# Roots of the norms spread by transposes of a broadcast column, residual and norm steps tile by tile, low-part products last

## The chip, the cores and the metric

The kernel is written by hand (each engine's queue is an explicit list of instructions with semaphores) and runs on one NeuronCore of a Trainium2 chip. The metric is the device time of one execution in microseconds, the median of several runs. Engines: TensorE (PE), VectorE (DVE), ScalarE (ACT), GpSimd (POOL) and SyncE (SP), which issues most of the loads.

## The reference

Two transformer blocks on x of 512 tokens by 1024 features, in float32. What matters here is how layers join. Four times the kernel computes, with y the output of a sublayer, g and g' gains (in the first block modulated by a conditioning vector):

```python
x = x + gate * rms_norm(y, g_post)           # rms_norm(a, g) = a * rsqrt(mean(a*a) + 1e-6) * g
h = rms_norm(x, g_pre) * (1 + scale) + shift # scale and shift in the first block only
```

The order is: norm of x, mixing sublayer of block 1 (pooling and dilated window attention), the two lines above, conv-FFN, the two lines, the mixing sublayer of block 2 (convolution, block attention, attention to a memory of 256 rows that has a norm of its own, gates), the two lines, conv-FFN, and the first of the two lines.

## The kernel before, in words

Activations lie transposed: features on the 128 partitions, 8 tiles (k = 0 to 7) of 128 x 512, tokens along the free axis. Weights come in units d = 0 to 135 of 256 columns; raw has two buffers (d mod 2). A product keeps float32 accuracy by splitting both operands into a high part (type fp32r) and a low part, the rest: ScalarE copies raw to WH (`split`), GpSimd subtracts to get WL (`cut`), and TensorE issues three matmuls for each (tile, half), high x high, high weight x low activation, low weight x high activation (`product`, line 1690). SyncE loads unit d+2 into the buffer of d once the cut of d is done.

`steps` (lines 443 to 576) is one list in the order of which every engine walks its own handlers, so it sets the order of each queue. `boundary` (line 510) is the part between a sublayer's last product and the next one's first:

1. Column sums. TensorE sums y squared and cross terms of y and x over the features with a stationary tile of squares and a moving column, so the sum of token p of group t stands at partition p, column 4t of PSUM bank 5.
2. `root_y`: ScalarE takes the square root of a column, VectorE the reciprocal, ScalarE makes four copies of the identity scaled by it (L893), and TensorE multiplies them by a matrix of ones (`spread`, L1676), which puts each token's factor on every partition, in bank 4. VectorE also derives from the cross sums the mean square of the new x (lines 1278 to 1282).
3. `root_x`: the same for the new x (L899, L1287, L902), into bank 6.
4. `blend`: for each tile VectorE makes the mix (L1299: y times gain times factor), adds it to x (L1304), and scales the new x (L1312) into dl; the three are staggered over tiles, so that tile k's mix goes with the add of k-1 and the scaling of k-2. ScalarE adds the shift (first boundary only, L920) and copies the high part hH (L922), GpSimd subtracts to hL (L752).
5. `twin` (line 1711): TensorE multiplies the tiles with the first two weight units of the next layer, in `TWIN_ORDER`, which takes the tiles of unit 0 and unit 1 alternately: 16 steps of 6 matmuls. Before a step of unit 0 it waits for hL of that tile.

`warm` issues matmuls of ones by ones into a bank that nothing reads: fillers while TensorE would be idle. Units of BY_ROWS (the two of each twin) are split and cut in two parts (tiles 0 to 3, 4 to 7); `("split", v + 2, 1)` is the second part of unit 1.

The first boundary lies at 277 to 326 us, the second at 676 to 714, the third at 1254 to 1296. The first norm (`norm`, around 36 to 42 us) and that of the memory (983 to 994) have no column sums: TensorE multiplies the squares by the full matrix of ones (L1642, so that all partitions hold all sums), VectorE picks each token's own with the identity and a reduction (L1343, L1345), and after the root scales four identities (L1350). Behind a boundary into a FFN, ScalarE's loop `up` waits for the first half of unit 0 (`pe_seg`), loads a function table, takes the bias (L1023) and splits the next unit; the twin is followed by TensorE's loop over the other units.

## Time and profile before

| | us |
|---|---|
| median of 3 runs (lowest, highest) | 1664.28 (1662.15, 1668.35) |
| the profiled execution's own time | 1666.63 |
| its span | 1664.8 |
| TensorE busy | 1555.7 (93%) |
| ScalarE, VectorE, GpSimd busy | 664.9, 588.2, 713.9 |
| TensorE's mean granted clock (share of full) | 0.967 |

### The profile page before, as it was taken

How to read it: one execution, taken by the hardware profiler on the slowest of the kernel's cores; microseconds unless marked ns; L12 is line 12 of the kernel's file. 1: busy time of each engine (PE TensorE's matmuls, PEld its weight loads, DVE VectorE, ACT ScalarE, POOL GpSimd, SP SyncE). 2: the span in 40 equal slices, each digit the busy share in tenths (PEclk: the TensorE clock that was granted, in tenths of full speed). 3: DMA queues.
4: the chain of work that ended last, by engine and by line, in shares of the span. 5: the costliest groups of instructions: out<-in, count | busy, mean ns of one | idle time of the engine just before them, and what ended most of it. 6: DMA issues, size and time to landing. Idle time of an engine off the chain costs nothing.

```text
span 1664.8 us, 19895 instructions
## 1 busy us (share of the span) xinstructions
PE 1555.7 (93%) x7670; PEld 1260.4 (76%) x7670; DVE 588.2 (35%) x928; ACT 664.9 (40%) x987; POOL 713.9 (43%) x608
## 2 busy tenths in 40 slices
PE   7899978899999999999989889999899999999996
PEld 4699757688888888788855568787687788887885
DVE  3665442523333100422034430342325555555001
ACT  2442453444444322322344443453333555544231
POOL 0467103535545544545411136335524554455442
PEclk8999987999999999999999999999999999999999
DMA  8463015322232223234210123122311222322221
GB/s 368 159 271 141 27 68 110 82 98 82 94 101 88 85 86 95 76 102 135 84 45 30 38 102 115 51 76 80 132 55 51 86 90 101 101 81 83 90 86 65
DMA packets 28491, 162.73 MB, mean 98 GB/s; under 512 B 4584, under 2 KB 4840, under 8 KB 13704
## 3 DMA queue, kind: packets, MB, share of 16 engines
q1 hardware_dynamic: 24960, 151.05, 26.4%
q10 hardware_dynamic: 3464, 10.74, 2.5%
q8 instruction: 47, 0.77, 0.2%
q14 instruction: 20, 0.16, 0.0%
HBM read 157.04 MB, written 4.74 MB: 97 GB/s over the span
## 4 chain that ended last, share of the span: by engine, by line
PE 70%; issue 10%; POOL 8%; DVE 6%; DMA 3%; ACT 2%; POOLq 0%; SPq 0%; ACTq 0%; DVEq 0%
PE ps L1693 60%; POOL WL L774 7%; DMA adaw<-w_ada_dram 2%; PE ps L1659 1%; PE ps L1902 1%; DMA raw<-w_up_dram 1%; PE ps L1916 1%; PE ps L1929 1%; DVE S L1584 1%; POOL WL L738 1%; DVE ps L1299 1%; DVE S L1571 1%; PE ps L1826 1%; DVE xT L1304 1%; DVE md L1574 0%
## 5 line engine op out<-in xcount | busy, mean ns | idle before, releaser
L738 POOL TENSOR_TENSOR WL<-raw,WH 128x512 fp32r<-128x512 f32 (+2 forms) x344 | 369.7, 1103 | 584.2 <-ACT WH L854 584.1
L1693 PE MATMUL ps<-hH,WH 128*128 128x512 f32 x1136 | 461.1, 406 | 22.2 <-POOL hL L752 9.3
L1693 PE MATMUL ps<-hL,WH 128*128 128x512 f32 x1136 | 453.9, 400 | 0.0
L1693 PE MATMUL ps<-hH,WL 128*128 128x512 f32 x1136 | 453.4, 399 | 0.0
L774 POOL TENSOR_TENSOR WL<-raw,WH 128x512 fp32r<-128x512 f32 x176 | 246.3, 1430 | 253.9 <-ACT WH L1014 253.9
L1693 PEld LDWEIGHTS ps<-hH,WH 128*128 128x128 f32 x1136 | 216.8, 191 | 79.5 <-issue 25.3
L1693 PEld LDWEIGHTS ps<-hH,WL 128*128 128x128 f32 x1136 | 216.6, 191 | 53.2
L1693 PEld LDWEIGHTS ps<-hL,WH 128*128 128x128 f32 x1136 | 216.8, 191 | 50.4
L854 ACT ACTIVATE WH<-raw 128x1024 fp32r<-128x1024 f32 (+3 forms) x172 | 148.1, 885 | 234.8 <-PE ps L1693 231.2
L1693 PE MATMUL ps<-hidH,WH 128*128 128x512 f32 x352 | 137.9, 392 | 1.1 <-POOL WL L774 1.1
L1693 PE MATMUL ps<-hidL,WH 128*128 128x512 f32 x352 | 137.0, 389 | 0.0
L1693 PE MATMUL ps<-hidH,WL 128*128 128x512 f32 x352 | 136.9, 389 | 0.0
L1470 DVE SCALAR_TENSOR_TENSOR act<-ps,vec,act 128x511 f32<-128x511 f32 x66 | 49.4, 748 | 173.2 <-ACT act L1023 173.2
L1014 ACT ACTIVATE WH<-raw 128x2048 fp32r<-128x2048 f32 x44 | 84.1, 1910 | 60.7 <-PE ps L1693 60.7
L1023 ACT ACTIVATE act<-ps,vec 128x512 f32<-128x512 f32 x66 | 50.1, 778 | 87.0 <-PE ps L1693 86.7
L1693 PEld LDWEIGHTS ps<-hidH,WH 128*128 128x128 f32 x352 | 66.1, 188 | 15.2 <-POOL WL L774 1.8
L1493 DVE TENSOR_TENSOR hidL<-act,hidH 128x512 f32 x44 | 70.1, 1631 | 21.2 <-ACT hidH L1043 21.2
L1693 PEld LDWEIGHTS ps<-hidH,WL 128*128 128x128 f32 x352 | 66.1, 188 | 13.8
L1693 PEld LDWEIGHTS ps<-hidL,WH 128*128 128x128 f32 x352 | 66.1, 188 | 13.4
L1571 DVE SCALAR_TENSOR_TENSOR S<-ps,W 128x128 f32<-128x128 f32 (+3 forms) x32 | 15.7, 491 | 127.5 <-PE ps L1902 127.5
L1023 ACT ACT_TABLE_LOAD x22 | 28.2, 1283 | 76.6 <-DVE hidL L1493 53.7
L1693 PE MATMUL ps<-WH,hpH 128*128 128x256 f32 x192 | 54.8, 285 | 0.8 <-DVE hpL L1374 0.5
(275 smaller groups left out, 2221.9 us busy)
## 6 DMA issues: line engine op xcount, KB each, us to landing
raw<-w_up_dram SPq DMA_DIRECT2D x44, 1024.0 KB, 4.9
raw<-w_in_dram SPq DMA_DIRECT2D x36, 1024.0 KB, 4.9
adaw<-w_ada_dram SPq DMA_DIRECT2D x20, 1024.0 KB, 7.1
raw<-w_down_dram SPq DMA_DIRECT2D x16, 768.0 KB, 4.2
raw<-w_down_dram SPq DMA_DIRECT2D x16, 640.0 KB, 3.9
adap<-w_ada_dram SPq DMA_DIRECT2D x4, 1024.0 KB, 18.1
xT<-x_dram ACTq DMA_DIRECT2D x2, 2048.0 KB, 10.2
raw<-w_mem_kv_dram SPq DMA_DIRECT2D x4, 1024.0 KB, 4.7
```

What stands on the lines that cost most here:

```text
L738: pool.tensor_tensor(WL[:, d % 2, ks, cols], raw[:, d % 2, ks, cols], WH[:, d % 2, ks, cols].bitcast(F32), ALU.subtract).then_inc(lo_done, 1)
L774: pool.tensor_tensor(WL[:, half, k:k + 2, :], raw[:, half, k:k + 2, :], WH[:, half, k:k + 2, :].bitcast(F32), ALU.subtract).then_inc(lo_do ...
L854: sc.activation(WH[:, d % 2, 0:nk, cols], raw[:, d % 2, 0:nk, cols], ACT.Copy).then_inc(hi_done, 1)
L1014: sc.activation(WH[:, half, :, :], raw[:, half, :, :], ACT.Copy).then_inc(hi_done, 2)
L1023: sc.activation(act[:, 2 * half + m, :], ps[:, 2 * half + m, :], ACT.Identity, bias=b, scale=w2).then_inc(seeded, 1)
L1299: ve.scalar_tensor_tensor(out=ps[:, 5 + 2 * (k % 2), :], in0=outputs[n][:, k, :], scalar=post_gains[n][:, k:k + 1], in1=ps[:, 4, :], op0=A ...
L1304: ve.tensor_tensor(xT[:, i, :], xT[:, i, :], ps[:, 5 + 2 * (i % 2), :], ALU.add).then_inc(x_added[0], 1)
L1470: ve.scalar_tensor_tensor(out=t[:, 1:S], in0=z[:, 0:S - 1], scalar=w1, in1=t[:, 1:S], op0=ALU.mult, op1=ALU.add).then_inc(dve_own, 1)
L1493: ve.tensor_tensor(hidL[:, bass.ds(j * 2 + m, 1), :], act[:, m:m + 1, :], hidH[:, bass.ds(j * 2 + m, 1), :].bitcast(F32), ALU.subtract).th ...
L1571: ve.scalar_tensor_tensor(out=S2[:, n % 2, 0:w], in0=ps[:, 4 + n % 2, 0:w], scalar=DH ** -0.5, in1=bias, op0=ALU.mult, op1=ALU.add).then_i ...
L1584: ve.tensor_scalar(S2[:, n % 2, 0:w], S2[:, n % 2, 0:w], md2[:, 2, n:n + 1], None, ALU.mult).then_inc(p2_scaled, 1)
L1693: mm = pe.matmul(out, lhs[x], rhs[y], start=(first and i == 0), stop=(last and i == 2))
```

## The change

- `norm`, first norm and memory: the sums are now columns too (`squares` uses a tile of squares as the stationary operand and one column of ones); ScalarE takes the root straight from PSUM, scale and epsilon in the same instruction, VectorE the reciprocal.
- All spreads: instead of scaled identities and ones, TensorE transposes the column of factors, read as 128 x 128 by repeating it, four transposes (two for the memory).
- `boundary`: the filler before the first spread goes, that before the blend has 4 matmuls, not 8; at the end of the kernel the filler before the spread goes.
- The second part of the split and cut of unit 1 moves from before the blend into it, on both engines behind tile 2.
- `blend` on VectorE: mix, add and scaling of one tile follow each other.
- `first_products`: in the twins and in the first units of the first and of the memory norm, each step issues its four matmuls with hH first, and only then waits for hL and issues the two with hL; the two halves of the unit so end one matmul apart.

```diff
-                    ("root_y", n), ("warm", 4, v + 1), ("spread_y", n), ("root_x", n), ("warm", 2, v + 1), ("spread_x", n),
-                    ("evac_y", n, KD - 1), ("split", v + 2, 1), ("warm", 8, v + 1), ("blend", n, nxt)]
+                    ("root_y", n), ("spread_y", n), ("root_x", n), ("warm", 2, v + 1), ("spread_x", n),
+                    ("evac_y", n, KD - 1), ("warm", 4, v + 1), ("blend", n, nxt)]
...
             def blend(n, nxt):                                    # GpSimd
                 for k in range(KD):
+                    if k == 3:
+                        cut(STAGE[n][1] + 1, 1)
...
-                sc.wait_ge(ry_ready, b)
-                for t in range(TT):
-                    ins = sc.activation(nt[:, 0, t * P:(t + 1) * P], ident, ACT.Identity, scale=ry_t[:, t:t + 1])
-                ins.then_inc(diag_y, 1)
...
             def norm(n):                                          # ScalarE
                 c = norm_source[n][1] // P
-                sc.wait_ge(var_ready, WHOLE[n] + 1)
-                sc.activation(nt[:, 0, 4:4 + c], nt[:, 0, 0:c], ACT.Sqrt).then_inc(std_ready, 1)
+                sc.wait_ge(weights_ready, 2)
+                sc.wait_ge(ss_added, KD * (SQUARED[n] + 1))
+                sc.activation(nt[:, 0, 0:c], ps[:, 5, 0:4 * c].rearrange("p (t i) -> p t i", i=4)[:, :, 0], ACT.Sqrt,
+                              bias=eps, scale=1.0 / D).then_inc(std_ready, 1)
 
             def blend(n, nxt):                                    # ScalarE
-                apply(nxt)
+                apply(nxt, 0, 3)
+                split(STAGE[n][1] + 1, 1)
+                apply(nxt, 3, KD)
...
+                for k in range(KD):                               # VectorE, blend
+                    d, m = output_tile(n, k)
+                    ve.wait_ge(banks_read[pair_of(d)], bank_use(d) + 1)
+                    ve.scalar_tensor_tensor(out=ps[:, 5 + 2 * (k % 2), :], in0=outputs[n][:, k, :], scalar=post_gains[n][:, k:k + 1],
+                                            in1=ps[:, 4, :], op0=ALU.mult, op1=ALU.mult).then_inc(mix_ready, 1)
+                    ve.wait_ge(mix_ready, KD * b + k + 1)
+                    ve.tensor_tensor(xT[:, k, :], xT[:, k, :], ps[:, 5 + 2 * (k % 2), :], ALU.add).then_inc(x_added[0], 1)
+                    ve.wait_ge(x_added[0], KD * b + k + 1)
+                    if k == 0:
+                        ve.wait_ge(rx_spread, b + 1)
+                    if k >= 4:
+                        wait_h(ve, nxt, k - 4)
+                    ve.scalar_tensor_tensor(out=dl[:, k % 4, :], in0=xT[:, k, :], scalar=gains[nxt][:, k:k + 1],
+                                            in1=ps[:, 6, :], op0=ALU.mult, op1=ALU.mult).then_inc(scaled, 1)
...
             def spread(n, i):                                     # TensorE
-                pe.wait_ge((diag_y, diag_x)[i], RESID[n] + 1)
+                pe.wait_ge((ry_ready, rx_ready)[i], RESID[n] + 1)
                 for t in range(TT):
-                    mm = pe.matmul(ps[:, 4 + 2 * i, t * P:(t + 1) * P], ones[:], nt[:, i, t * P:(t + 1) * P], start=True, stop=True)
+                    mm = pe.transpose(ps[:, 4 + 2 * i, t * P:(t + 1) * P], (ry_t, rx_t)[i][:, t:t + 1].broadcast_to([P, P]), ident)
...
+            def first_products(outs, s, n, k, last):
+                hi, lo = (memH, memL) if n == N_MEM else (hH, hL)
+                cols = [slice(m * P, (m + 1) * P) for m in range(2)]
+                pe.wait_ge(h_hi, KD * SPLITS[n] + k + 1)
+                for o, c in zip(outs, cols):
+                    pe.matmul(o, WH[:, s, k, c], hi[:, k, :], start=(k == 0), stop=False)
+                    pe.matmul(o, WL[:, s, k, c], hi[:, k, :], start=False, stop=False)
+                wait_h(pe, n, k)
+                done = [pe.matmul(o, WH[:, s, k, c], lo[:, k, :], start=False, stop=last) for o, c in zip(outs, cols)]
+                return done
```

## Rows read from the trace of the kernel before

**Rows 1.** The page, chain that ended last: shares by engine.
```profile
PE 70%; issue 10%; POOL 8%; DVE 6%; DMA 3%; ACT 2%; POOLq 0%; SPq 0%; ACTq 0%; DVEq 0%
```

**Rows 2.** Timeline of TensorE, third boundary: start, duration, instruction, [idle before, releaser].
```profile
1258.45 1.03 PE L1670 MATMUL ps<-small,prod 128*128 128x1 f32 x8
...
1260.47 1.16 PE L1676 MATMUL ps<-nt,ones 128*128 128x128 f32 x8
...
1267.94 0.76 PE L1693 MATMUL ps<-hH,WH 128*128 128x512 f32 x1 [2.81 <-POOL hL L752]
...
1295.68 0.79 PE L1693 MATMUL ps<-hH,WH 128*128 128x512 f32 x1 [3.56 <-POOL WL L774]
```

**Rows 3.** Timeline of ScalarE, third boundary.
```profile
1259.14 1.28 ACT L893 ACTIVATE nt<-ident_t,small 128x128 f32<-128x128 f32 x4 [0.25 <-DVE small L1273]
...
1265.80 0.63 ACT L922 ACTIVATE hH<-dl 128x512 fp32r<-128x512 f32 x1 [2.25 <-DVE dl L1312]
...
1285.96 1.28 ACT L1023 ACT_TABLE_LOAD   x1 [8.03 <-PE ps L1693]
```

**Rows 4.** Timeline of VectorE, third boundary.
```profile
1260.00 0.16 DVE L1282 TENSOR_TENSOR small<-ps,small 128x4 f32<-128x4 f32 x1
1260.63 0.18 DVE L1287 RECIPROCAL small<-small 128x4 f32<-128x4 f32 x1 [0.48 <-ACT small L899]
1261.66 1.41 DVE L1299 SCALAR_TENSOR_TENSOR ps<-y,vec,ps 128x512 f32<-128x512 f32 x2 [0.85 <-PE ps L1676]
...
1265.03 0.74 DVE L1312 SCALAR_TENSOR_TENSOR dl<-xT,vec,ps 128x512 f32<-128x512 f32 x1
```

**Rows 5.** Timeline of GpSimd, third boundary.
```profile
1263.63 2.50 POOL L731 TENSOR_TENSOR WL<-raw,WH 128x512 fp32r<-128x512 f32 x2 [2.62 <-ACT WH L848]
1266.51 1.28 POOL L752 TENSOR_TENSOR hL<-dl,hH 128x512 fp32r<-128x512 f32 x1 [0.38 <-ACT hH L922]
```

**Rows 6.** Timeline of TensorE, first and second boundary.
```profile
285.09 1.85 PE L1670 MATMUL ps<-small,prod 128*128 128x1 f32 x8
...
325.78 0.74 PE L1693 MATMUL ps<-hH,WH 128*128 128x512 f32 x1 [3.60 <-POOL WL L774]
...
689.91 0.47 PE L1693 MATMUL ps<-hH,WH 128*128 128x512 f32 x1 [2.81 <-POOL hL L752]
```

**Rows 7.** Timeline of TensorE, transposes of the first attention (half clock, then full).
```profile
215.42 2.25 PE L1837 MATMUL ps<-ident_t,S 128*128 128x128 f32 x8 [6.25 <-DVE S L1444]
...
220.92 0.66 PE L1837 MATMUL ps<-ident_t,S 128*128 128x128 f32 x4
```

**Rows 8.** Timeline of VectorE, first and second boundary.
```profile
287.45 0.16 DVE L1282 TENSOR_TENSOR small<-ps,small 128x4 f32<-128x4 f32 x1
...
680.96 0.16 DVE L1282 TENSOR_TENSOR small<-ps,small 128x4 f32<-128x4 f32 x1
```

**Rows 9.** Timeline of VectorE, end of the kernel: a mix and the add that needs it.
```profile
1654.19 0.75 DVE L1329 SCALAR_TENSOR_TENSOR ps<-yff,vec,ps 128x512 f32<-128x512 f32 x1
1654.98 0.69 DVE L1332 TENSOR_TENSOR xT<-xT,ps 128x512 f32<-128x512 f32 x1
```

**Rows 10.** Windows: PE, PEld, DVE, ACT, POOL busy (instructions), granted clock, DMA share, GB/s.
```profile
286.00:289.00 3.00, 3.00 (x15) 3.00 (x15) 0.68 (x4) 2.16 (x8) 0.23 (x1) 0.50 0.49 54
...
1268.00:1271.00 3.00, 3.00 (x7) 2.38 (x8) 3.00 (x6) 0.98 (x2) 1.95 (x2) 0.50 0.74 303
```

**Rows 11.** Timeline of TensorE, memory norm (three rows) and first norm (last row).
```profile
984.10 4.93 PE L1642 MATMUL ps<-sq,ones 128*128 128x256 f32 x16 [1.45 <-ACT sq L862]
991.21 1.03 PE L1649 MATMUL ps<-nt,ones 128*128 128x128 f32 x4 [2.19 <-DVE nt L1350]
994.02 0.55 PE L1693 MATMUL ps<-bufAH,WH 128*128 128x256 f32 x1 [1.78 <-DVE bufAL L1366]
...
39.53 2.08 PE L1649 MATMUL ps<-nt,ones 128*128 128x128 f32 x8 [1.27 <-DVE nt L1350]
```

**Rows 12.** DMA issues from 240 to 330 us: count, KB each, median us to landing.
```profile
raw<-w_up_dram SPq DMA_DIRECT2D x5, 1024.0 KB, 16.7
```

More of the change, by code:

```diff
@@ L1641, in squares @@
                 pe.wait_ge(sq_ready, KD * SQUARED[n] + k + 1)
-                pe.matmul(ps[:, 5, 0:w], ones[:], sq[:, k % 2, 0:w], start=(k == 0), stop=(k == KD - 1)
-                          ).then_inc(ss_added, 1)
+                for t in range(w // P):
+                    mm = pe.matmul(ps[:, 5, 4 * t:4 * t + 1], sq[:, k % 2, t * P:(t + 1) * P], ones[:, 0:1],
+                                   start=(k == 0 and t == 0), stop=(k == KD - 1 and t == w // P - 1))
+                mm.then_inc(ss_added, 1)
             def norm(n):
-                pe.wait_ge(diag_ready, WHOLE[n] + 1)
+                if n == N_PRE1:
+                    pe.wait_ge(ident_loaded, 16)
+                pe.wait_ge(inverse_ready, WHOLE[n] + 1)
                 for t in range(norm_source[n][1] // P):
-                    mm = pe.matmul(ps[:, 4, t * P:(t + 1) * P], ones[:], nt[:, 1, t * P:(t + 1) * P], start=True, stop=True)
+                    mm = pe.transpose(ps[:, 4, t * P:(t + 1) * P], nt[:, 0, 8 + t:9 + t].broadcast_to([P, P]), ident)
                 mm.then_inc(rstd_ready, 1)
@@ L1719, in twin @@
                         pe.wait_ge(lo_done, 4 * d + k // 2 + 1)
-                    if w == 0:
-                        wait_h(pe, nxt, k)
-                    for m in range(2):
-                        cols = slice(m * P, (m + 1) * P)
-                        mm = product(ps[:, 2 * w + m, :], (WH[:, w, k, cols], WL[:, w, k, cols]),
-                                     (hH[:, k, :], hL[:, k, :]), k == 0, k == KD - 1)
+                    for mm in first_products([ps[:, 2 * w + m, :] for m in range(2)], w, nxt, k, k == KD - 1):
                         if k == KD - 1:
@@ L1766, in seg @@
                         if d in first_of:
-                            wait_h(pe, first_of[d], k)
-                        for half in (0, 1) if d in first_of else (m,):
-                            cols = slice(half * P, (half + 1) * P)
-                            mm = product(ps[:, 2 * p + half, 0:w], (WH[:, s, k, cols], WL[:, s, k, cols]),
+                            first, mm = first_products([ps[:, 2 * p + i, 0:w] for i in range(2)], s, first_of[d], k, k == nk - 1)
+                            if k == nk - 1:
+                                first.then_inc(pe_seg, 1)
+                        else:
+                            cols = slice(m * P, (m + 1) * P)
+                            mm = product(ps[:, 2 * p + m, 0:w], (WH[:, s, k, cols], WL[:, s, k, cols]),
                                          (src[0][:, k0 + k, :], src[1][:, k0 + k, :]),
                                          k == 0 and q == 0, k == nk - 1 and (not down or q == 3))
-                            if d in first_of and k == nk - 1 and half == 0:
-                                mm.then_inc(pe_seg, 1)
                 else:
```

49 lines of the change are left out of this document (5 added, 44 removed).

## The prediction

> **What bounds the kernel now.** I read the page's chain of waits first, then each engine's timeline around the places that the diff touches. TensorE carries 70% of the chain [rows 1]. So a change pays only where TensorE has to wait for the vector work between two layers, and the reader is to look at three boundaries (post-norm into next pre-norm), at the memory norm, the first norm and the end.
>
> At the third boundary TensorE does its last column sums at 1258.45 (ending 1259.48), a filler step, the first spread at 1260.47, then more filler and the second spread, and then nothing until the first real product at 1267.94, released by GpSimd's low part [rows 2]. Behind it lies a chain: root and four copies of the identity scaled by the root on ScalarE (1.28 us), first mix on VectorE at 1261.66, first normalised tile at 1265.03, its high part at 1265.80, its low part at 1266.51 [rows 2 to 5]. From 1267.94 the 96 products of the twin run without a hole until 1292.12 (1295.68 less 3.56 of idling) [rows 2]. The first boundary ends alike, with 3.60 us idle before 325.78; at the second the products start at 689.91 [rows 6].
>
> **The change part by part.**
>
> *Spreads.* The four ScalarE copies go (1.28 us each root), and so does the filler ahead of the first spread; four matmuls in two passes (8 records, 1.16 us) become four transposes. The diff's own transpose of a broadcast column is not in the trace; the nearest rows are transposes of ordinary tiles: four take 0.66 us at full clock, and eight 2.25 us, so 1.12 for four, at half clock [rows 7]. Bounds for four: 0.6 (ordinary) to 2.3 (the old spread's eight records at half clock, twice 1.16); I take 0.66 and 1.12.
>
> *Where mixing starts.* VectorE still needs the x root in program order: the sum is ready when the instruction of 1260.00 ends (1260.16); ScalarE, no longer busy with copies, takes the root at once (0.3), the reciprocal 0.18 (as at 1260.63) [rows 4]; the first mix starts at 1260.70, not 1261.66. The spread, 1259.48 to 1260.14, is no longer what it waits for. At the other boundaries the same instruction starts at 287.45 and 680.96 [rows 8], which gives first mixes at 288.16 and 681.66.
>
> *Three steps in a row.* A dependent step starts 0.79 us after the one before it (1654.19 to 1654.98), an independent one 0.66 (half of the pair of 1.41 at 1261.66, less overlap) [rows 4, 9]. Mix, add, scale of one tile then begin 0.79 and 0.72 apart, and the next tile 0.66 later: a period of 2.17 us against 1.92 before. The first scaled tile starts 1.51 after the first mix, against 3.37 before (1261.66 to 1265.03) [rows 4]. So it starts at D = 1262.2 (was 1265.03) and 683.2 at the second; at the first the x spread at half clock holds it to 290.1 (sums end 286.94 [rows 6], then 1.12, four filler records 0.96, 1.12). The last tile starts 15.2 after D, near 1277.4, about a microsecond later than before; TensorE's order needs it only at D+18, so that costs nothing as long as TensorE is behind.
>
> By the Trainium skill, page "VectorE: DVE Perf Modes", section "The DRAIN you can't avoid", a pipe empties after each instruction whatever one does and "the semaphore costs nothing extra here". By that the period would stay at 1.92 and the time fall by about another 0.4 us a boundary; the 0.79 against 0.66 of this trace says otherwise, and I go by the trace.
>
> *Products with low parts last.* Four of six products of a tile need only the high part. It is ready at D+1.45 (the 0.77 from 1265.03 to 1265.80, plus 0.63), the low part at D+2.85 (GpSimd 1.28) [rows 3 to 5]; before, TensorE started 2.91 after D. First and third boundary pay a price: the first tile's half signals one product pair later (2 x 0.23 = 0.5 us), and ScalarE's table load at 1285.96 waits for that signal [rows 3].
>
> *The second cut moved into the blend.* GpSimd's 2.50 us [rows 5] comes after its third low part (D+7.2), so the fourth is ready at D+11.0, the fifth 12.3, the sixth 13.6, the last 18.0. ScalarE's copy (1.05) fits in its gaps. Behind the cut wait the load of the next-but-one weights (the buffer comes free at about D+9.7) and four low parts.
>
> *TensorE against this supply.* At 0.233 us a product, 1.4 a step: first step D+1.5 to 3.4 (waits 0.4 for the low part), then 4.8, 6.2, 7.7, 9.1; the step of the fourth tile has its high products by 10.0 and waits 1.0 for the cut, ends 11.5; the other 10 steps run through to D+25.5. Before, the twin lasted 24.2 from 1267.94, of which 1.5 is a stretch at half clock, 0.50 in 1268 to 1271 after the idle time [rows 2, 10]. If such a stretch comes early again, the wait for the cut absorbs it, so the sum doesn't lean on the clock.
> - third: 1262.2 + 25.5 = 1287.7 against 1292.1: 4.4, less 0.5 for the signal: 3.9
> - second: 683.2 + 25.5 = 708.7 against 689.91 + 24.1 = 714.0: 5.3 (no signal price; there ScalarE waits for both halves)
> - first: a shift on ScalarE adds 0.77 to each tile: 290.1 + 26.3 = 316.4 against 322.2: 5.8, less 0.5: 5.3
>
> Together 14.5. The FFN and projection loops behind are kept full by TensorE, so the start carries to the end.
>
> *Memory norm.* Squares run as columns (4.93 us now, my estimate 0.5 less); then TensorE idles 2.19 for three VectorE steps, a root and the scaled identities, spreads in 1.03 and waits 1.78 more [rows 11]. Now the root follows the squares directly, behind the table load (1.28, [rows 3]) that ScalarE does anyway: 0.9 earlier; two transposes save 0.4; starting on the high part 0.7. Together 2.5 with the squares; I take 2.4 (0.9 to 3.3).
>
> *First norm.* The spread at 39.53 waits 1.27 for VectorE [rows 11]. Without it TensorE goes on at 38.3 and spreads by 39.4, not 41.6: 2.2. The row product behind then has more of its 7.5 us at half clock: 1.3 left (0 to 2.2).
>
> *The end.* The copies (1.28) and 0.5 of the spread go: 1.8.
>
> **Sum:** 14.5 + 2.4 + 1.3 + 1.8 = 20.0 us. The profiled execution took 1666.63 (span 1664.8), which gives 1646.6; it lies 2.4 above the median of 1664.28, and with the same gain the median becomes 1644.3. I say 1644.5.
>
> **Rivals.**
> *A: the clock.* 3 us windows show half clock from 286 to 289 although TensorE was busy 3.00 of 3.00 with column sums and fillers [rows 10]; so it is half (1.2 of 2.4 GHz) for all that work, and the diff leaves 12 of 28 filler records and 8 of 16 spread records a boundary. If the twins begin with a longer stretch at half clock than the waits absorb, each further 3.1 us costs 1.45: three boundaries 4.4, time 1649. Against it: the idle gap shrinks from 2.81 to about 1.2.
> The Trainium skill ("TensorE: Matmul & The Clock Gate", section "PE-mode transpose") says that transposes don't count as busy for the clock; by that this rival gets likelier. Transposes between other matmuls ran at full clock here (0.66 for four [rows 7]), which neither shows nor refutes it.
> *B: a late load.* At the first boundary the load freed by the moved cut (290.1 + 10.5 = 300.6) meets the bias rows' store; with the 16.7 us that such loads took there [rows 12] it is there at 317.3, just as ScalarE wants it (about 317.4); I expect less, since the store is over by then. Any more comes off the 5.3: time up to 1650.
> *C: slower.* Half clock through the whole twins: 96 products at 0.427 instead of 0.233 are 18.6 us each, 56 for three; 56 less 20 gives 1700. It decides from the point where 36% of each twin (20/56) is slow. For it: the half-clock row above; against it: in each boundary before, the clock came back some 3 us after products flowed.
> *D: the gains don't add.* Only the spreads' shortening survives (about 1 us at each of three first mixes, the norms 3.7, the end 1.8: 8.5), since GpSimd's cut sets the twin's end, later than I think: 1655.8.
>
> **How the numbers follow.** Main case 68%, A 14%, B 8%, D 6%, C 4%. Main alone 1641 to 1648 (memory 0.9 to 3.3, first 0 to 2.2, one less slow stretch a boundary). The range goes to 1653 to take in A and B, and to 1640. Half a percent is 8.3 us, about what a measurement tells from none: below 1656 lie main, A, B and some of D: 0.90; same 0.06; slower 0.04.
>
> **What would show it.** TensorE's first product at D+1.5 (1.5 before its low part) and its largest hole in the twin at the fourth tile, some 1 us, released by GpSimd's low part; VectorE's mixes 2.17 apart; ScalarE's table load 4 to 5.5 us earlier from the start of its boundary; four records per spread. Wrong if four transposes take over 1.5 us at full clock, if half clock is seen beyond D+7, or if the first loop step stalls on a load.

## The result, and the profile after

The changed kernel takes 1648.2 us in the median of four runs (1646.7 to 1649.7) and the kernel before 1665.2 on the same chip (1662.2 to 1668.4). The ratio is 0.989, with a 95% interval of 0.987 to 0.991. The two profiled executions took 1666.63 and 1646.69 us, with spans of 1664.8 and 1644.9: 19.9 us apart where the medians are 17.0 apart. The forecast was 1644.5 us (1640 to 1653), with a sum of 20.0 for the profiled pair; it had started from a median of 1664.3 for the kernel before.

The page of the changed kernel: busy time of each engine, and the chain by engine (it answers [rows 1]).

```profile
PE 1548.0 (94%) x7644; PEld 1256.5 (76%) x7644; DVE 585.0 (36%) x917; ACT 656.3 (40%) x959; POOL 714.3 (43%) x608
...
PE 70%; issue 10%; POOL 9%; DVE 6%; DMA 3%; ACT 2%; POOLq 0%; SPq 0%; ACTq 0%; DVEq 0%
```

The chain is made of the same engines in nearly the same shares. So the page alone tells nothing of where 20 us went, and one has to go into the three boundaries.

Timeline of TensorE at the third boundary, changed kernel (answers [rows 2]; times are 14 us earlier, since that much had been gained before it).

```profile
1245.07 0.63 PE L1656 MATMUL ps<-ident_t,small 128*128 128x128 f32 x4
...
1246.48 1.11 PE L1656 MATMUL ps<-ident_t,small 128*128 128x128 f32 x4 [0.34 <-DVE small L1281]
1247.38 1.92 PE L1668 MATMUL ps<-ones 128*128 128x128 f32 x8
1249.39 0.70 PE L1682 MATMUL ps<-hH,WH 128*128 128x512 f32 x1
...
1258.79 0.74 PE L1685 MATMUL ps<-hL,WH 128*128 128x512 f32 x2 [0.70 <-POOL hL L751]
...
1277.55 0.79 PE L1673 MATMUL ps<-hH,WH 128*128 128x512 f32 x1 [4.03 <-POOL WL L773]
```

A spread is four records now. The first takes 0.63 us for all four, at full clock; the second comes behind a wait of 0.34 us and takes 1.11, at half clock, and so does the filler behind it. The forecast had both at full clock here. The only hole inside the twin products is at the fourth tile, released by GpSimd's low part. Ahead of the FF loop TensorE idles 4.03 us, where it was 3.56.

ScalarE at the same boundary (answers [rows 3]); the first row is the root of the y norm, from which I count every stretch below.

```profile
1244.35 0.26 ACT L887 ACTIVATE small<-ps,small 128x4 f32<-128x4 f32 x1 [0.20 <-PE ps L1639]
...
1248.62 0.63 ACT L916 ACTIVATE hH<-dl 128x512 fp32r<-128x512 f32 x1 [1.92 <-DVE dl L1299]
...
1267.83 1.28 ACT L1017 ACT_TABLE_LOAD   x1 [3.38 <-PE ps L1685]
```

VectorE (answers [rows 4]): the x root's reciprocal, then mix, add and scale of the first tile, and the next tile's mix.

```profile
1246.24 0.18 DVE L1281 RECIPROCAL small<-small 128x4 f32<-128x4 f32 x1 [0.37 <-ACT small L893]
1246.34 0.74 DVE L1290 SCALAR_TENSOR_TENSOR ps<-y,vec,ps 128x512 f32<-128x512 f32 x1
1247.11 0.69 DVE L1293 TENSOR_TENSOR xT<-xT,ps 128x512 f32<-128x512 f32 x1
1247.84 0.75 DVE L1299 SCALAR_TENSOR_TENSOR dl<-xT,vec,ps 128x512 f32<-128x512 f32 x1
1248.50 0.75 DVE L1290 SCALAR_TENSOR_TENSOR ps<-y,vec,ps 128x512 f32<-128x512 f32 x1
```

GpSimd (answers [rows 5]): low part of tile 0 (tiles 1 and 2 follow at 2.17 us steps), the moved cut, the first two low parts behind it.

```profile
1249.33 1.29 POOL L751 TENSOR_TENSOR hL<-dl,hH 128x512 fp32r<-128x512 f32 x1 [2.61 <-ACT hH L916]
...
1254.93 2.55 POOL L728 TENSOR_TENSOR WL<-raw,WH 128x512 fp32r<-128x512 f32 x2
1257.44 2.55 POOL L751 TENSOR_TENSOR hL<-dl,hH 128x512 fp32r<-128x512 f32 x2
```

The spacings 0.77, 0.73 and 0.66 add up to the forecast period of 2.17 us (1248.50 less 1246.34 is 2.16), and D, the start of the first scaled tile, is 1247.84: with the 14.3 us gained before it, the forecast's 1262.2 becomes 1247.9.

TensorE at the first and second boundary (answers [rows 6]).

```profile
285.65 1.09 PE L1656 MATMUL ps<-ident_t,small 128*128 128x128 f32 x4
...
290.87 0.47 PE L1682 MATMUL ps<-hH,WH 128*128 128x512 f32 x1 [0.71 <-ACT hH L916]
...
300.27 0.73 PE L1685 MATMUL ps<-hL,WH 128*128 128x512 f32 x2 [0.70 <-POOL hL L751]
...
319.06 0.79 PE L1673 MATMUL ps<-hH,WH 128*128 128x512 f32 x1 [4.06 <-POOL WL L773]
...
678.99 0.77 PE L1682 MATMUL ps<-hH,WH 128*128 128x512 f32 x1 [0.40 <-ACT hH L916]
```

TensorE at the first norm (first row), the memory norm (three rows) and the end (last row): these answer [rows 11] and, for the end, the filler and spread of the kernel before.

```profile
38.05 1.09 PE L1629 MATMUL ps<-ident_t,nt 128*128 128x128 f32 x4
...
973.02 5.16 PE L1619 MATMUL ps<-ones,sq 128*128 128x1 f32 x32 [1.45 <-ACT sq L861]
978.99 0.69 PE L1629 MATMUL ps<-ident_t,nt 128*128 128x128 f32 x2 [0.81 <-DVE nt L1325]
980.79 0.55 PE L1682 MATMUL ps<-bufAH,WH 128*128 128x256 f32 x1 [1.11 <-ACT bufAH L916]
...
1632.91 0.65 PE L1656 MATMUL ps<-ident_t,small 128*128 128x128 f32 x4 [0.57 <-DVE small L1267]
```

**Where the 19.9 us came from.** I lay the two traces side by side at equal landmarks and note how far the changed kernel is ahead: 1.14 us before the first boundary, 6.72 at the first loop's start (gain 5.58), 5.65 at the end of the projections behind that loop (a loss of 1.07), 10.96 behind the second boundary (5.3), 13.88 behind the memory norm (2.8), 14.28 before the third boundary (0.4), 18.13 at the second loop's start (3.86), 18.10 at the loop's end, 19.9 at the end of the span (1.8). The loss of 1.07 is the one entry that no term of the forecast has. Windows of the changed kernel behind the first loop's start show what it is (columns as in [rows 10]).

```profile
319.00:321.00 2.00, 1.95 (x5) 1.58 (x6) 2.00 (x2) 0.16 (x1) 2.00 (x2) 0.50 0.52 86
...
323.00:325.00 2.00, 2.00 (x6) 1.57 (x5) 0.00 (x0) 0.00 (x0) 1.79 (x2) 0.53 0.10 37
```

The granted clock is 0.50 (1.2 of 2.4 GHz) for some 5.7 us behind the idle stretch. The kernel before has 0.52 and 0.63 in the two windows behind its own loop start, then 1.00:

```profile
325.78:327.78 2.00, 2.00 (x5) 1.63 (x6) 2.00 (x2) 0.11 (x1) 2.00 (x2) 0.52 0.54 94
327.78:329.78 2.00, 2.00 (x8) 1.54 (x7) 0.13 (x1) 0.00 (x0) 2.00 (x2) 0.63 0.95 397
```

### The profile page after: what moved, and what is told of

Read it like the earlier page. It is cut to its first block, busy times and chain, and to the rows that moved or that the text cites. A ratio compares the mean times of both kernels' runs of the same rounds, so it can differ in the third digit from the quotient of the medians.

```text
span 1644.9 us, 19792 instructions
## 1 busy us (share of the span) xinstructions
PE 1548.0 (94%) x7644; PEld 1256.5 (76%) x7644; DVE 585.0 (36%) x917; ACT 656.3 (40%) x959; POOL 714.3 (43%) x608
## 4 chain that ended last, share of the span: by engine, by line
PE 70%; issue 10%; POOL 9%; DVE 6%; DMA 3%; ACT 2%; POOLq 0%; SPq 0%; ACTq 0%; DVEq 0%
PE ps L1673 58%; POOL WL L773 7%; DMA adaw<-w_ada_dram 2%; PE ps L1639 1%; PE ps L1889 1%; DMA raw<-w_up_dram 1%; PE ps L1903 1%; PE ps L1916 1%; DVE S L1560 1%; POOL WL L735 1%; DVE dl L1299 1%; DVE xT L1293 1%; DVE ps L1290 1%; PE ps L1813 1%; PE ps L1685 1%
## 5 line engine op out<-in xcount | busy, mean ns | idle before, releaser
L1673 PE MATMUL ps<-hH,WH 128*128 128x512 f32 x1024 | 414.6, 405 | 10.0 <-POOL WL L773 8.1
L1673 PE MATMUL ps<-hL,WH 128*128 128x512 f32 x1024 | 407.7, 398 | 0.0
L1673 PE MATMUL ps<-hH,WL 128*128 128x512 f32 x1024 | 407.6, 398 | 0.0
L1673 PEld LDWEIGHTS ps<-hH,WH 128*128 128x128 f32 x1024 | 194.7, 190 | 61.1 <-issue 15.6
L1673 PEld LDWEIGHTS ps<-hH,WL 128*128 128x128 f32 x1024 | 194.2, 190 | 47.7
L1673 PEld LDWEIGHTS ps<-hL,WH 128*128 128x128 f32 x1024 | 194.7, 190 | 45.2
```

Of the source, the lines that this page charges most:

```text
L1673: mm = pe.matmul(out, lhs[x], rhs[y], start=(first and i == 0), stop=(last and i == 2))
```

## The experiments

A kernel's timed runs here spread over 3 to 7 us, and two medians of the unaltered changed kernel, taken at different times, are 1648.2 and 1646.3. Parts worth 1 to 3 us can't be read from that. So I read each experiment in its trace, over three stretches that begin at the root of the y norm on ScalarE: to the first product of the FF loop at the first and third boundary, to the first product behind the twins at the second. In us:

```
                    first   second  third   end    median
before              40.52   34.33   37.05   14.3   1665.2
changed             34.94   29.01   33.20   12.5   1648.2
changed again       34.94   29.02   33.20   12.5   1646.3
low part first      34.45*  29.95   33.68   12.5   1647.1
staggered steps     37.08   31.19   34.55   12.7   1649.2
scaled identities   37.08   32.11   35.77   15.3   1658.6
cut before          33.32*  28.75   32.94   12.5   1645.5
old norms           34.93   29.00   33.20   12.5   1648.2
no fillers          34.01*  29.32   33.54   12.5   1646.1
first half early    33.64   29.57   31.93   12.5   1647.4
best, no filler     33.66   28.76   31.93   12.5   1643.8
best, filled        32.70*  28.75   31.93   12.5   1636.3
```

"End" is from the last y root to the end of the span. At a star TensorE did the last column sums at 2.4 GHz and not at 1.2: the x root came 1.56 instead of 2.38 us after the y root, and D, the start of the first scaled tile, 3.49 instead of 4.44. So 0.95 us of the difference at a star is the clock's, and a part is read there from D on. The unaltered kernel repeats its stretches within 0.01 us.

**The changed kernel again.**

> The changed kernel, unaltered, beside the others on the same chip: 1648 us in the median, 17 us (1.0%) under the kernel before. Everything below is told against this run.

Measured: 1646.3 us in the median of four, ratio 0.989 (0.986 to 0.991).

**Low part first.**

```
-  wait(high k); for o, c: WH*hi, WL*hi
-  wait(low k);  for o, c: WH*lo
+  wait(high k); wait(low k)
+  for o, c: WH*hi, WH*lo, WL*hi
```

> One part undone: the product with a tile's low part is no longer last. Each first product again waits for high and low part of its tile, and then goes high*high, high*low of the operand, low*high of the weights for each half, as before. Main theory (the part is worth the distance between a tile's high and low part, once per boundary, because the tiles arrive slower than TensorE uses them up and the last tile ends the stretch): the first product of a boundary starts 1.4 us later (D+2.85 in place of D+1.45, D the start of the first scaled tile); at the end of the stretch 0.9 us of it is left at each of three boundaries, less the 0.5 us by which the signal after the first half comes earlier in this order at two of them, and 0.7 us at the memory norm: 2.4 us in all over the changed kernel, 1650.5 us. Rival (TensorE never waits for a low part except at the fourth tile, and what is late at the end is the weights' cut, not the tile): no change, within 0.5 us. Rival of the clock: a longer idle stretch ahead of the first product makes the half-clock stretch behind it longer, and each boundary costs 1 to 2 us more than the main theory says: 5 to 7 us.

Measured, first product of the third boundary:

```profile
1251.50 0.47 PE L1683 MATMUL ps<-hH,WH 128*128 128x512 f32 x1 [1.64 <-POOL hL L751]
```

The first product waits for GpSimd and starts 1.37 us later after the y root than in the changed kernel (1251.50 less 1245.09, against 5.04). The stretches are 0.94 longer at the second and 0.48 at the third; at the first it is 0.46, counted from D. From the spread of the memory norm to its first product it is 2.47 in place of 1.80. Together 2.5 us, where the main theory had 2.4. The rival (no change) falls. The clock rival falls too: nothing near 2 us is added at a boundary. The median is only 0.7 above the unaltered one, and the trace shows why totals can't tell. In this execution the first FF loop ran at 2.4 GHz from its start and took 352.3 us to the next y root, not 354.8; but from 840 to 854 us, in work that the change doesn't touch, the granted clock was 0.50 and 0.54 where the changed kernel had 1.00, and nearly 5 us went there.

**Staggered steps.**

```
-  for k: mix k; add k; scale k
+  for k in range(KD + 2): mix k; add k-1; scale k-2
```

> One part undone: VectorE's three steps of a tile (mix, add of the residual, scale) are staggered over the tiles again, as before, so that no step directly follows the one it depends on. Main theory: the first scaled tile comes 1.86 us later (two mixes, two adds ahead of it in place of one each), the period of a tile falls from 2.17 to about 1.92 us, so that the eighth tile comes near where it did, and the twin products end about 1.4 us later at each boundary, since TensorE starts 1.9 us later and makes up only part of it: 4.2 us in all, 1652.3 us. Rival (only the last tile matters, the period's gain pays for the later start): within 0.5 us of the changed kernel. Rival of the clock as in the run before: the longer idle stretch adds another 1 to 2 us per boundary.

Measured, third boundary:

```profile
1252.32 0.47 PE L1689 MATMUL ps<-hH,WH 128*128 128x512 f32 x1 [1.95 <-ACT hH L916]
```

The first product is 1.86 us later after the y root, as worked out (6.90 against 5.04). The third stretch grows by 1.35, near the 1.4 of the theory, the second by 2.18 and the first by 2.14: 5.7 in all against 4.2. The larger two are the clock's: idle for 2.42 us ahead of the first product at the first boundary, TensorE ran at half clock from 291.8 to 295.2 us (high products of 0.63 us in place of 0.40); at the second the granted clock is 0.83 over the 10 us from 680. The rival "only the last tile matters" falls. So each theory had a part: 1.4 from the order, and 0.8 more where a slow stretch followed that the waits for tiles did not absorb. An idle stretch of this length doesn't always bring one: at the third boundary TensorE had idled for 1.95 us, and the products ran at full clock.

**Scaled identities.**

```
-  transpose(ps, ry[:, t:t+1].broadcast_to([P, P]), ident)
+  ScalarE: nt[:, t, :] = ident * ry[:, t:t+1]      (4 copies)
+  TensorE: matmul(ps, ones, nt[:, t, :])
```

> One part undone: the roots of the residual norms are spread by scaled identities (ScalarE writes four of them, TensorE multiplies them by ones) in place of the transposes of a broadcast column, at the three boundaries and at the end; first norm and memory norm stay as changed, and nothing is added to the filler products. Main theory: ahead of the first mix this costs 0.96 us at the third boundary, about 2 us and 2.4 us at the second and first (their ones products run at the half clock), and 1.8 us at the end, all of it on the path that sets the start of the mixes: about 7 us in all, 1655 us. Rival (the spread of the roots is hidden behind VectorE's other work at the boundaries, only the end shows it): 1.8 us. Rival: the scaled identities keep TensorE idle longer, the clock falls in the boundary where it did not, and the sum is over 9 us.

Measured, third boundary: the two spreads, and the windows.

```profile
1251.38 1.73 PE L1667 MATMUL ps<-nt,ones 128*128 128x128 f32 x8 [0.99 <-ACT nt L894]
...
1253.75 1.75 PE L1667 MATMUL ps<-nt,ones 128*128 128x128 f32 x8
```

```profile
1249.00:1252.00 3.00, 2.01 (x17) 1.93 (x17) 1.20 (x7) 2.31 (x8) 2.50 (x2) 0.97 0.00 0
1252.00:1255.00 3.00, 3.00 (x16) 3.00 (x15) 1.44 (x2) 1.51 (x5) 0.00 (x0) 0.50 0.00 0
```

The stretches are 2.14, 3.10 and 2.57 longer and the end 2.72: 10.5 us, and the median is 12.3 higher (ratio to the kernel before 0.996, 0.995 to 0.998). The main theory said 7, "over 9 because TensorE idles and its clock falls" was the second rival, and that it is: without the filler ahead of the y spread TensorE waits 0.99 us for ScalarE's copies, and both spreads run at half clock, 1.7 us each, where the kernel before had 1.16 [rows 2]. The kernel before, its y root and its filler:

```profile
1258.63 0.26 ACT L889 ACTIVATE small<-ps,small 128x4 f32<-128x4 f32 x1 [0.20 <-PE ps L1659]
```

```profile
1259.34 1.14 PE L1688 MATMUL ps<-ones 128*128 128x128 f32 x8
```

Its filler delayed nothing: with it the y spread starts at 1260.47, 1.84 us after the root, and here without it also 1.84 after (1251.38 less 1249.54), since both wait for the copies. It bought full clock for both spreads. So 10.5 us is not the share of the transposes in the 20: this experiment takes them out without giving the filler back. Their share is better read up to the first mix, which starts 5.33, 4.04, 3.04 and 3.04 us after the y root in the kernel before (three boundaries and the end) and 2.80, 1.99, 1.99 and 1.22 in the changed one: 7.5 us, the 7 of the main theory, and still the largest part.

**The cut ahead of the blend.**

```
   root_x, spread_x, evac_y(last),
+  split and cut of the second half,
   blend:
-     behind tile 2 (the third): split and cut of the second half
```

> One part undone: the second half of the next weights' split and its cut by GpSimd stand ahead of the mixes again, not behind the third tile. Counted from the start of the root of the y norm on ScalarE, where the changed kernel takes 34.94 us to the first product of the FF loop at the first boundary, 29.0 us to the end of the twin products at the second and 33.20 us at the third. Theory (the move is worth nothing: the hole of 0.70 us before the fourth tile's low part goes, but the first low part comes about a microsecond later, as ScalarE's 1.05 us and GpSimd's 2.55 us are then ahead of it, and the tile rate of 2.17 us sets the end either way): each stretch within 0.3 us of the changed kernel's. Rival (the cut ahead of the blend keeps GpSimd from the first low parts, and this is carried through): 1 to 2.5 us more per boundary. Rival (the hole is lost time that comes back in full): 0.7 us less per boundary. In the total all three lie within 0 to +7 us, and only the first is no change.

Measured: 0.26 us less at the second and third boundary. At the first it is 1.62 less, of which 0.95 is the clock of the column sums. The other 0.67 is not: in both traces the granted clock is 1.00 from the first product of the first boundary on. First product and wait for the first low part there, and the same wait at the third boundary:

```profile
286.98 0.47 PE L1678 MATMUL ps<-hH,WH 128*128 128x512 f32 x1 [0.85 <-ACT hH L912]
...
288.38 0.73 PE L1681 MATMUL ps<-hL,WH 128*128 128x512 f32 x2 [0.23 <-POOL hL L749]
```

```profile
1248.25 0.73 PE L1681 MATMUL ps<-hL,WH 128*128 128x512 f32 x2 [0.98 <-POOL hL L749]
```

The hole at the fourth tile goes everywhere, 0.70 us, but the first low part comes 0.85 us later. At the third boundary TensorE waits 0.98 us for it; at the first, where the first product itself starts later after D, only 0.23, and the hole comes back nearly in full. So the theory (nothing, within 0.3) stands at the second and third boundary, and the second rival (0.7 back in full) at the first, in one execution. Moving the cut into the blend bought nothing and lost 1.2 us over the three. The first rival falls.

**The old norms.**

```
   first norm and memory norm:
-  column sums [128x1], root, reciprocal, transposes
+  sums into a full bank [128xw], fix-up, root, scaled identities * ones
```

> One part undone: first norm and memory norm are summed and spread as before (sums by ones into a full bank, VectorE's fix-up, four or two scaled identities by ones); the order with the low part last stays, and the boundaries stay as changed. Main theory: at the first norm the first product comes 1.2 us later, at the memory norm the first product comes 1.9 us later (in the kernel before, from the start of the sums' last record to the first product: 2.19 us of waiting and 1.03 us of ones products, where the changed kernel has 0.81 and 0.69, and before that sums of 128x256 in place of 128x1): 3 us in all. Rival (what is late at the memory norm is the cut of the weights and not the norm, the gain that was seen there came from the clock): under 1 us at the memory norm, 1.2 us in all.

Measured, the two spreads.

```profile
39.51 2.08 PE L1636 MATMUL ps<-nt,ones 128*128 128x128 f32 x8 [1.27 <-DVE nt L1337]
...
980.60 1.21 PE L1636 MATMUL ps<-nt,ones 128*128 128x128 f32 x4 [2.19 <-DVE nt L1337]
```

Memory norm: from the end of the sums to the first product it is 4.51 us in place of 2.61, so 1.9 as expected. But the sums themselves take 4.93 us here and in the kernel before, at a granted clock of 1.00, and 5.16 to 6.55 us as one-column products in the other twelve traces, with a mean clock of 0.54 to 0.87 over them. So the new form gives back 0.2 to 1.6 us of its gain, more or less from one execution to the next. First norm: the spread ends 2.45 later (41.59 against 39.14), and the first product behind the next row product 2.2 to 3.4 later than in the three runs beside it. That is about twice the 1.2 expected: I had let the row product's half-clock stretch take a microsecond back, and here it didn't. The rival (under 1 us at the memory norm) falls.

**No fillers at the boundaries.**

```
-  ("root_x", n), ("warm", 2), ("spread_x", n), ("evac_y", n, 7), ("warm", 4), blend
+  ("root_x", n), ("spread_x", n), ("evac_y", n, 7), blend
```

> One thing taken away that the change touched in its place and count: TensorE's filler products between the two spreads and behind the second, at the three boundaries (nothing reads them). Counted as in the runs beside it, from the root of the y norm. Theory (TensorE is idle there anyway, the fillers are hidden and only guard the clock, which falls at the first boundary with them too): 0 to 0.5 us more per boundary, all of it from transposes and first products at the half clock. Rival (the fillers are what keeps the clock at 2.4 GHz at the second and third boundary): there the granted clock in the 6 us behind the first product is near 0.5 to 0.7, where the changed kernel has about 1.0, and the stretch is 1.4 us or more longer at each. Rival (the fillers delay the x spread or the first product): 0.3 to 0.5 us less per boundary.

Measured, third boundary (TensorE busy 0.14 of 2 us, then products at half clock for 4 us).

```profile
1244.00:1246.00 2.00, 0.14 (x1) 0.17 (x2) 1.93 (x4) 0.63 (x1) 0.21 (x1) 0.50 0.02 4
...
1248.00:1250.00 2.00, 2.00 (x6) 1.52 (x6) 1.97 (x3) 0.57 (x2) 1.25 (x1) 0.53 0.00 0
```

0.31 us more at the second and 0.34 at the third boundary; at the first no difference (0.02), counted from D. The first product starts where it did, 5.04 after the y root. The clock is indeed worse, as the first rival says, but it costs 0.3 and not 1.4: VectorE delivers a tile each 2.17 us, so that the products wait for the fourth tile's low part anyway (0.70 us in the changed kernel); in this trace that hole is gone, and the slow products have filled it and most of what else TensorE waits. This is what I had called absorption, measured.

**The first unit's first half earlier.**

```
-  ..., (0, 6), (1, 3), (0, 7), (1, 4), ...      last tile: both halves high, both low
+  ..., (0, 6), (0, 7), (1, 3), (1, 4), ...      last tile: half 0 high, low, signal; half 1
```

> One thing added to the changed kernel: of the twin products at a boundary, the last tile of the first unit is taken one step earlier in the order, (0,7) ahead of (1,3), and at a unit's last tile the first half's three products (and its signal) stand ahead of the second half's. What the first product of the FF loop waits for is a chain that begins at that signal (table load, two evacuations, the split on ScalarE, the cut on GpSimd) and took 9.7 us in the changed kernel, with TensorE idle for 4.0 us at its end. A sum over the rows of the changed kernel (tile k's high part at D+1.5+2.17k, its low part 1.4 us after, the cut of 2.55 us behind the third, 0.2335 us for a product) gives the signal at D+18.34 in place of D+19.73, and the last twin product at D+26.05 in place of D+25.57. Theory (the chain sets the loop's start): at the first and third boundary 1.4 us less (33.5 and 31.8 us), TensorE's idle time before the loop about 2.2 us, at the second boundary, which has no such chain behind it, 0.5 us more (29.5 us); in all 2.3 us less. Rival (the chain is held by the second unit or by VectorE, not by this signal): no change at the first and third, 0.5 us more at the second. Rival of the clock: the shorter idle stretch leaves TensorE's clock up, and the first loop steps run up to 2.5 us faster, twice.

Measured, first loop product of the third boundary:

```profile
1278.31 0.79 PE L1673 MATMUL ps<-hH,WH 128*128 128x512 f32 x1 [2.21 <-POOL WL L773]
```

Stretches 33.64, 29.57 and 31.93, idle time 2.21: expected were 33.5, 29.5, 31.8 and 2.2. What the loop's start waits for is the chain behind that signal, not TensorE. The clock rival falls: both loops still start with 3.3 us at half clock. The median did not show the 2 us (1647.4), and neither did the profiled execution, which had the slow clock at 841.5 to 855 us as in the run with the low part first (granted clock 0.50 over 847 to 855).

**Two probes of the clock.** TensorE idles before 36.3 us at the start of the kernel, at 1.2 GHz. In the one probe it transposes there, in the other it multiplies.

```
+  for _ in range(40): transpose(ps[:, 7, 0:P], ident, ident)
   or
+  for _ in range(20): matmul(ps[:, 7, 0:P], ones, ones)
```

> A probe of the clock in the changed kernel: in the idle stretch of TensorE at the start (about 31.7 to 36.3 us, the granted clock there is 1.2 GHz) 40 transposes of the identity are issued; nothing reads them. They take 0.27 us each at 1.2 GHz and 0.16 at 2.4 (from 1.09 and 0.65 us for four). Theory A (transposes leave the clock as it is): all 40 run at 1.2 GHz, 10.9 us, and what follows starts about 6 us later than in the changed kernel. Theory B (they raise it as products do): the granted clock reaches 1.00 within them, as in the twin probe with products, and 40 take under 9 us. The Trainium skill (TensorE: Matmul & The Clock Gate, the section on the PE-mode transpose) states A.

> The twin of the probe with transposes: at the same place 20 ordinary fp32 products of ones by ones (128x128, 40 records, since each leaves two). A record takes 0.24 us at 1.2 GHz and 0.12 at 2.4. Both theories: the granted clock rises to 2.4 GHz within them after 4 to 7 us, and the 40 records take 6 to 8 us. If the clock stays at 1.2 GHz here too (9.6 us), the probe tells nothing on transposes.

Measured, transposes, then products, each with windows.

```profile
32.52 6.80 PE L1673 MATMUL ps<-ident_t 128*128 128x128 f32 x40
```

```profile
34.00:36.00 2.00, 2.00 (x12) 2.00 (x11) 1.93 (x3) 0.00 (x0) 1.43 (x2) 0.50 1.00 422
36.00:38.00 2.00, 2.00 (x15) 2.00 (x15) 0.52 (x3) 0.00 (x0) 0.00 (x0) 0.73 1.02 430
38.00:40.00 2.00, 2.00 (x22) 2.00 (x20) 0.00 (x0) 0.00 (x0) 0.00 (x0) 1.00 1.00 422
```

```profile
29.72 6.23 PE L1673 MATMUL ps<-ones 128*128 128x128 f32 x40
```

```profile
32.00:34.00 2.00, 2.00 (x17) 2.00 (x16) 0.82 (x2) 0.00 (x0) 0.62 (x1) 0.78 1.03 434
34.00:36.00 2.00, 1.95 (x18) 1.75 (x16) 1.93 (x3) 0.00 (x0) 0.00 (x0) 1.00 0.99 422
```

Nothing but transposes runs on TensorE from 32.5 to 39.2, and the clock goes from 0.50 to 1.00 within them, near 37 us; with the products it does so near 33. That is theory B. TensorE had been busy with one-column products at half clock before, in both probes, and had not idled. Each probe ran once. The forecast had weighed the Trainium skill's rule ("TensorE: Matmul & The Clock Gate", section "PE-mode transpose") that transposes don't count for the clock; for these fp32 transposes the trace disagrees.

**The best version, filled and not.** Both kernels have the cut ahead of the blend at all boundaries and the earlier signal at the first and third. They differ only in this:

```
   twin(d0)
+  for _ in range(9): matmul(ps[:, 7, 0:P], ones, ones)
   FF loop
```

> Three things on the changed kernel: the earlier signal of the first unit's first half at the first and third boundary (at the second the old order), the split and cut ahead of the blend at all three, and nine filler products (ones by ones, 18 records, about 2.1 us at 2.4 GHz, nothing reads them) behind the twin products, in the idle stretch before the FF loop's first product at the first and third boundary. From the runs so far: 1.3 us less at each of first and third boundary by the signal, 0.26 us less at each of three by the cut, 3.3 us in all by these two. Theory of the clock (the half-clock stretch at the head of each FF loop, 3.3 to 5.6 us long in the traces, follows from the idle stretch of 2.2 to 4.1 us before it): with the fillers the granted clock is 1.00 in the first 6 us of both loops, worth 1.7 us each against the same kernel without fillers: 6.5 to 7 us under the changed kernel, 1640 us. Rival (ones by ones does not hold the clock, or the clock falls later in the loop all the same): no gain by the fillers, 1643.5 us. Rival (the fillers delay the loop's first product): up to 0.5 us more per loop.

> The run above without its filler products: the earlier signal at the first and third boundary and the cut ahead of the blend at all three. Counted from the root of the y norm: 33.4 us at the first boundary, 28.75 at the second, 31.65 at the third (the changed kernel: 34.94, 29.0, 33.2), the head of each FF loop at 1.2 GHz for about 3.3 us. In the total 3.3 us under the changed kernel, 1644 us; rival (the cut ahead of the blend and the earlier signal do not add, because tile and not cut sets the seventh tile's low part): 2.6 us.

Measured, filled kernel: fillers and first loop product of the third boundary, and the window behind it.

```profile
1267.20 2.17 PE L1860 MATMUL ps<-ones 128*128 128x128 f32 x18
1269.57 0.49 PE L1671 MATMUL ps<-hH,WH 128*128 128x512 f32 x1 [0.20 <-POOL WL L773]
```

```profile
1270.00:1272.00 2.00, 2.00 (x11) 1.59 (x10) 1.73 (x4) 0.12 (x1) 1.80 (x2) 1.00 0.68 164
```

The kernel without fillers, first loop:

```profile
316.32:318.32 2.00, 2.00 (x5) 1.62 (x6) 1.54 (x2) 0.82 (x2) 2.00 (x2) 0.53 0.56 102
```

Without fillers: 1643.8 us (ratio 0.987, 0.985 to 0.989), stretches 33.66, 28.76, 31.93. Against the changed kernel 2.8 us in the stretches: the rival's number (2.6), since behind the earlier signal the cut's place adds nothing at the first and third boundary. With fillers: 1636.3 us, ratio 0.984 (0.982 to 0.985), the fastest of all. Both loops run at 1.00 from the first product and are 1.52 us shorter each (352.3 against 353.8, 353.5 against 355.0), close to the 1.7 expected. That is 3.0 of the 6.4 us between the two profiled executions; the other 3.4 lie in places that the fillers don't touch (1.6 before the first boundary, 1.0 in it, by the clock of the column sums, 0.8 between the second and the third), and whether they would come back in each run stays open. The medians are 7.5 apart, of five runs each (1634.2 to 1639.4 against 1638.3 to 1645.0); the traces account for 3.0 of that.

## Why the prediction was right

The total came out as 20.0 forecast and 19.9 measured for the profiled pair. The terms bear that out one by one, but that the sums meet to a tenth is luck: the parts gave 0.5 us more than the terms, 0.4 us more came between the memory norm and the third boundary, where no term is, and 1.07 us were lost at the head of the first loop, which no term has either.

**Spreads as transposes.** Taken at 0.66 us for four at full clock and 1.12 at half; measured 0.63 to 0.65, and 1.06 to 1.11. A broadcast column as the stationary side costs nothing extra.

**Where mixing starts.** Third boundary: forecast 1260.70, less 14.28 is 1246.42; measured 1246.34. At the first the x spread sets D, as said, but 0.4 earlier (288.55 against 290.1 less 1.14), because groups of four half-clock records follow each other 0.86 us apart, not 1.12: the rows' durations overlap.

**Three steps in a row.** Period 2.17 forecast and measured; the experiment puts the part at 1.35 us where the clock is quiet.

**The drain.** By the Trainium skill ("VectorE: DVE Perf Modes", section "The DRAIN you can't avoid"), where the semaphore costs nothing extra, the period would have stayed at 1.92. The trace gave 2.17, as [rows 9] had said.

**The twin products.** First product at D+1.55, hole at the fourth tile 0.70 (said: about 1.0), twin's end at D+25.7 (said: 25.5; at the first boundary D+26.4 against 26.3). A slip in it had no effect: five low parts stand behind the cut, not four. ScalarE's table load came 5.6 us earlier after the y root at the first boundary and 3.9 at the third (said: 4 to 5.5). From it 9.72 us to the loop at the third boundary and 9.74 at the first, as in the kernel before (9.72 and 9.75), so no load came late (rival B).

**The boundaries** together: 5.58 + 5.3 + 3.86 = 14.7 against 14.5. **Memory norm** 2.8 against 2.4, with one term wrong: the column sums are not 0.5 shorter than the old ones but 0.2 longer in this execution (5.16 against 4.93), and up to 1.6 in others. **First norm** 1.14 at the first boundary against 1.3, though for the wrong reason: the part itself is worth about 2.5, and a stretch at half clock between 167 and 172 us took 1.6 of it back in this execution. **End** 1.8 against 1.8. The sum of these is 20.5. The parts undone one at a time come to about 22 us (2.5, 5.7, 10.5, less 1.2, and 1.9 + 2.5 for the norms); they are not independent, as the scaled identities without their filler show.

**What the forecast didn't have** is the 1.07 lost at the head of the first loop. I had seen that the signal came later in relation to the twin's end and charged its 0.5 us, but not that TensorE's idle time there grows by the same amount (3.60 to 4.06) and that a half-clock stretch follows it. How long this is differs from execution to execution: to the next y root the first loop takes 352.3 us in one of thirteen traces, 353.8 in five and 354.8 in seven, with nothing changed in it. The kernel before had 353.8 and the changed one 354.9 (the fillers of the best version give 352.3). It does not look like chance alone. Of the 18 loops that had 4.03 to 4.07 us of idle time ahead of them, 12 began with 5 to 5.8 us at half clock; of the 8 with 2.2 to 3.6 us, none did (seven had about 3.3 us, one none). That speaks for the longer idle stretch as part of the price of the change, about 1.1 us in two loops of three, though no run varies it alone; in the profiled execution only the first loop paid it.

**The clock (rival A)** is most likely what lies between 19.9 and 17.0, and in the 3.7 us by which the median missed 1644.5; that is not shown. What speaks for it: long executions go with a low clock (the kernel before, seven runs: 1657.6 us at a mean granted clock of 0.971, 1668.2 at 0.963), and two medians of the changed kernel are 2 us apart. It never cost what rival A charges in the boundaries: in the changed kernel the first products ran at half clock for at most a microsecond, and where they did so for longer, without the fillers, the waits for tiles took up all but 0.3 us. By its letter one sign of being wrong did occur, half clock beyond D+7; it was at the head of the loops, behind the twins, where the kernel before has it too. **Rivals C and D** fall: in the changed kernel half clock ended by D+3 at every boundary, and the cut does not set the twin's end (its experiment moves it by 0.3 to 0.7).

## What to carry to other kernels

When parts are worth a few microseconds and runs spread as much, count stretches in the trace from one engine's event to the next event that everything waits for; they repeat to 0.01 us where medians differ by 2. An edit that shortens TensorE's work in front of a fixed chain on other engines lengthens the idle stretch behind it, and the slow clock that follows can cost again: fill the stretch with products that nothing reads, sized to end just before the chain does (2.17 us in 2.4 here, worth 1.5 us a time), or start the chain earlier. Where a later supply sets the pace, as at the boundaries here, the same fillers are worth only 0.3 us.

## What the hardware showed that I had not expected

- VectorE's instruction may start before the one in front of it has ended, when nothing ties them: the mix starts at 1246.34, the reciprocal before it runs from 1246.24 to 1246.42.
- Forty fp32 transposes in a row brought TensorE from 1.2 to 2.4 GHz, as products did.
- TensorE ran at 1.2 GHz while fully busy, mostly with one-column sums, from 24 to 28 us (4.00 of 4.00 us busy, granted clock 0.50), and with column sums ahead of the first boundary; in four of fourteen traces the latter ended at 2.4 GHz.
- The probe with products took 1643.5 us in its single run, against 1646.3 and 1648.2 for the unaltered kernel at other times, though it adds work: its first norm's spread is at 37.29 us, not 38.05, and the first product behind the next row product at 54.44, not 56.88, with the clock up from 34 us. One run can't settle whether that is a gain.
